# Grouped-query attention: the value product three steps behind its scores, the low half two steps behind

## The reference

```python
def gqa_dense(q, k, v, sink=None):
    scale = HEAD_DIM ** -0.5
    def attend(qb):
        s = jnp.einsum('bqhgd,bkhd->bhgqk', qb, k, preferred_element_type=F32) * scale
        ...
            p = jax.nn.softmax(s, axis=-1)
        return jnp.einsum('bhgqk,bkhd->bqhgd', p.astype(v.dtype), v)
    return sweep_queries(attend, (q,))
...
        elif kind == 1:
            q, k, vv, g_c = gqa_project(hc, gqa_w_in[j])
            q, k = rms_norm(q, gqa_q_norm[j]), rms_norm(k, gqa_k_norm[j])
            o_c = gqa_dense(q, k, vv)
            ...
            k_all = jnp.concatenate([cache_gqa_k[:, j], k_l], axis=1)
            v_all = jnp.concatenate([cache_gqa_v[:, j], v_l], axis=1)
            o_l = gqa_dense(q_l, k_all, v_all)
```

## Time and profile before

| | us |
|---|---|
| median of 3 runs | 4803.26 |
| lowest, highest | 4797.92, 4811.78 |
| the profiled execution | 4798.57 |
| its span | 4796.8 |
| TensorE busy in the span | 4166.2 (87%) |
| VectorE busy | 2699.8 (56%) |
| ACT busy | 2399.6 (50%) |
| GpSimd busy | 1178.5 (25%) |

### The profile page before, as it was taken

One profiled execution on the slowest core, in us unless ns is written; L12 is line 12 of the kernel. 1 busy time (PEld: TensorE's weight loads), 2 busy tenths in 40 slices (PEclk: granted clock), 3 DMA queues, 4 the chain that ended last, 5 costly groups with the idle time before them and its releaser, 6 DMA issues. The chain is left out here.

```text
span 4796.8 us, 63498 instructions
## 1 busy us (share of the span) xinstructions
PE 4166.2 (87%) x21676; PEld 2101.5 (44%) x21676; DVE 2699.8 (56%) x3564; ACT 2399.6 (50%) x3114; POOL 1178.5 (25%) x785
## 2 busy tenths in 40 slices
PE   5996899999958979999995978888859868999996
PEld 1443344444434444444443545555434433444443
DVE  4323577767345547777625516777453336777753
ACT  3324366666333227777723215666433245777752
POOL 1010143334211114444411201232210102444431
PEclk7997899999979979999997988999979988999998
DMA  4125422222111332222111333333111253222211
GB/s 177 51 70 156 112 60 69 62 63 59 31 47 49 95 92 70 69 69 69 46 31 44 102 96 80 87 83 88 45 40 56 67 152 91 50 49 49 49 35 57
DMA packets 372746, 343.63 MB, mean 72 GB/s; under 512 B 252576, under 2 KB 288992, under 8 KB 370944
## 3 DMA queue, kind: packets, MB, share of 16 engines
q1 hardware_dynamic: 372608, 341.81, 25.6%
HBM read 250.51 MB, written 91.23 MB: 71 GB/s over the span
## 5 line engine op out<-in xcount | busy, mean ns | idle before, releaser
L352 PE MATMUL bank<-H_hilo,w_hilo 128*128 128x512 f16 (+1 forms) x6336 | 1155.1, 345 | 25.9 <-DVE w_hilo L721 25.9
L1213 DVE TENSOR_REDUCE max_parts<-bank 128x1 f32<-128x512 f32 (+2 forms) x1536 | 953.5, 649 | 248.5 <-PE bank L1164 208.6
L1397 ACT ACTIVATE p_f<-bank 128x1024 f32<-128x1024 f32 (+2 forms) x768 | 741.8, 966 | 668.0 <-PE bank L1354 651.6
L1354 PE MATMUL bank<-q_slots,k_slots 96*128 96x512 f16 (+7 forms) x3968 | 957.8, 372 | 0.8 <-ACT p_hi L1401 0.6
L1469 DVE TENSOR_TENSOR p_lo<-p_f,p_hi 128x1024 f16<-128x1024 f32 (+2 forms) x624 | 738.2, 1186 | 341.1 <-ACT p_hi L1401 338.0
L352 PEld LDWEIGHTS bank<-H_hilo,w_hilo 128*128 128x128 f16 x6336 | 622.3, 98 | 558.3 <-DVE w_hilo L721 27.5
L1401 ACT ACTIVATE p_hi<-bank 128x1024 f16<-128x1024 f32 (+2 forms) x768 | 739.0, 962 | 0.0
L1164 PE MATMUL bank<-k_slots,q_slots 96*128 96x512 f16 (+4 forms) x1536 | 527.6, 381 | 110.5 <-DVE max_parts L1213 73.4
L1326 PE MATMUL bank<-p_hi,v_hi_ones 128*128 128x512 f16 (+2 forms) x1568 | 582.2, 372 | 10.2 <-DVE o_f L1449 6.8
L1328 PE MATMUL bank<-p_hi,v_lo_zeros 128*128 128x512 f16 (+2 forms) x1568 | 581.3, 371 | 0.0
L1330 PE MATMUL bank<-p_lo,v_hi_ones 128*128 128x512 f16 (+2 forms) x1568 | 579.2, 370 | 0.0
(11 more groups left out here) (140 smaller groups left out, 3856.1 us busy)
## 6 DMA issues: line engine op xcount, KB each, us to landing
ada_w<-in_w_ada SPq DMA_DIRECT2D x48, 768.0 KB, 5.6
k_slots<-k_gqa SPq DMA_DIRECT2D x96, 224.0 KB, 4.5
gate<-z_ring SPq DMA_DIRECT2D x32, 640.0 KB, 2.9
gate_rows<-gate SPq DMA_DIRECT2D x64, 320.0 KB, 3.9
q_slots<-q_mla SPq DMA_DIRECT2D x64, 240.0 KB, 3.1
k_mla<-hilo_out SPq DMA_DIRECT2D x64, 224.0 KB
k_slots<-k_mla SPq DMA_DIRECT2D x64, 224.0 KB, 4.3
v_hi_ones<-v_scratch SPq DMA_DIRECT2D x64, 224.0 KB, 2.9
```

Source lines behind the costliest of these rows:

```text
L352: ins = pe.matmul(dst, lhs(a, k), rhs(b, k), start=(k == 0 and n == 0), stop=(k == nk - 1 and n == 2))
L1213: dve.tensor_reduce(mx[:, par, t, c:c + 1], MB[(b * NE + k) % 2][:, 0:n], AX.X, ALU.max).then_inc(s_red.h, 1)
L1354: ins = pe.matmul(dst, lhs, rhs, start=(m == 0), stop=(m == len(ops) - 1), skip_group_check=swa)
L1397: act.activation(p32[:, p % 2, 0:cols], src, ACT.Exp, scale=scale).then_inc(s_p32.h, 1)
```

## The change

For layer 1 (`kind == 1`) a number `behind` is 3, for the others 2, as before. Where TensorE issued the value product of p-2 it issues that of p - behind; VectorE takes the low half of e = p - behind + 1 instead of p-1; the end of a unit on ACT, VectorE and the runs behind the last step move by the same one step. `ring(n)` gives a list of slots: n of them, or n + 1 over a stretch at the end of the pair where the number of steps asks for it. `p_hi` and `p_lo` get ring(4) in layer 1, which is 4 slots and for the last ten steps 5. `p_f32` gets ring(2). Since 26 is divisible by 2, ring(2) comes out with the two slots that there were. GpSimd's low halves and the layers 0, 2 and 3 stay as they were; line numbers grow by 6 or 7 behind the edit.

```diff
-        fours = next(n for n in range(P2) if (P2 - 4 * n) % 3 == 0)
-        slot = [p % 3 for p in range(P2 - 4 * fours)] + [p % 4 for p in range(4 * fours)]
-        back = [next(d for d in range(1, P2) if slot[p - d] == slot[p]) for p in range(P2)]
+        behind = 3 if kind == 1 else 2
+
+        def ring(n):
+
+            wide = next(m for m in range(P2) if (P2 - (n + 1) * m) % n == 0)
+            slots = [p % n for p in range(P2 - (n + 1) * wide)] + [p % (n + 1) for p in range((n + 1) * wide)]
+            return slots, [next(d for d in range(1, P2) if slots[p - d] == slots[p]) for p in range(P2)]
+        slot, back = ring(behind + 1)
+        ph = sb("p_hi", [P, max(slot) + 1, 1024], F16)
+        pl = sb("p_lo", [P, max(slot) + 1, 1024], F16)
+        slot32, back32 = ring(2) if behind > 2 else ([p % 2 for p in range(P2)], [2] * P2)
+        p32 = sb("p_f32", [P, max(slot32) + 1, 1024], F32)
...
-                        if (p >= 2 or not first) and (p < P2 or last):
-                            pv(i, p - 2)
+                        if (p >= behind or not first) and (p < P2 or last):
+                            pv(i, p - behind)
...
-                            if above_zero(g - 1):
-                                wait_lo(act, i, p - 2)
-                            act.activation(p32[:, p % 2, 0:cols], src, ACT.Exp, scale=scale).then_inc(s_p32.h, 1)
+                            if above_zero(g - back32[p] + 1):
+                                wait_lo(act, i, p - back32[p])
+                            act.activation(p32[:, slot32[p], 0:cols], src, ACT.Exp, scale=scale).then_inc(s_p32.h, 1)
...
-                        q = (p - 2) % P2
+                        q = (p - behind) % P2
...
-                    e = p - 3
+                    e = p - behind - 1
...
-                        if p <= P2 and not (first and p == 0) and (p - 1) % P2 % NS not in pooled:
-
-                            q = (p - 1) % P2
+                        e = p - behind + 1
+                        if e < P2 and not (first and e < 0) and e % P2 % NS not in pooled:
+
+                            q = e % P2
```

More of the change, by code:

```diff
@@ L993, in attention @@
         G = sb("gate_rows", [P, TOK], F32)
-        p32 = sb("p_f32", [P, 2, 1024], F32)
-        ph = sb("p_hi", [P, 4, 1024], F16)
-        pl = sb("p_lo", [P, 4, 1024], F16)
         mx = sb("max_parts", [P, 2, 4, 3], F32)
@@ L1338, in body @@
                 def body(i, first, last):
-                    for p in range(P2 + 2):
+                    for p in range(P2 + behind):
                         if p < P2:
@@ L1385, in body @@
                 def body(i, first, last):
-                    for p in range(P2 + (2 if last else 0)):
+                    for p in range(P2 + (behind if last else 0)):
                         if p < P2:
@@ L1405, in body @@
                                     copy_rows(act, i * 2 + b + 1, 1 - b, k)
-                        if p < 2 and first:
+                        if p < behind and first:
                             continue
-                        q = (p - 2) % P2
+                        q = (p - behind) % P2
                         u = steps[q % NS][0]
                         if q % NS == last_of[u]:
-                            un = 3 * (q // NS) + u - (6 if p < 2 else 0)
+                            un = 3 * (q // NS) + u - (6 if p < behind else 0)
                             b = q // NS
                             nq = units[u][1]
-                            act.wait_ge(s_av.h, s_av.base + i * P2 + p - 1)
+                            act.wait_ge(s_av.h, s_av.base + i * P2 + p - behind + 1)
                             if above_zero(i * 6 + un - 1):
@@ L1454, in body @@
                     i_first[0] = first
-                    for p in range(P2 + (3 if last else 0)):
+                    for p in range(P2 + (behind + 1 if last else 0)):
                         b = p // NS
@@ L1459, in body @@
                             take_entry(dve, i * 2 + b + 1, 1 - b, k)
-                        if p <= P2 and not (first and p == 0) and (p - 1) % P2 % NS not in pooled:
-                            q = (p - 1) % P2
+                        e = p - behind + 1
+                        if e < P2 and not (first and e < 0) and e % P2 % NS not in pooled:
+                            q = e % P2
                             cols = steps[q % NS][2]
-                            g = i * P2 + p - 1
+                            g = i * P2 + e
                             dve.wait_ge(s_ph.h, s_ph.base + g + 1)
@@ L1468, in body @@
                                 dve.wait_ge(s_av.h, s_av.base + g - back[q] + 1)
-                            dve.tensor_tensor(pl[:, slot[q], 0:cols], p32[:, q % 2, 0:cols], ph[:, slot[q], 0:cols],
+                            dve.tensor_tensor(pl[:, slot[q], 0:cols], p32[:, slot32[q], 0:cols], ph[:, slot[q], 0:cols],
                                               ALU.subtract).then_inc(s_pl.h, 1)
@@ L1528, in p_lo @@
                         pool.wait_ge(s_av.h, s_av.base + g - back[p] + 1)
-                    pool.tensor_tensor(pl[:, slot[p], 0:cols], p32[:, p % 2, 0:cols], ph[:, slot[p], 0:cols],
+                    pool.tensor_tensor(pl[:, slot[p], 0:cols], p32[:, slot32[p], 0:cols], ph[:, slot[p], 0:cols],
                                        ALU.subtract).then_inc(s_pp.h, 1)
```

## The result

The changed kernel takes 4904.79 us (median of 4 runs, 4902.59 to 4912.17) against 4804.24 for the kernel before in the same comparison: a ratio of 1.0211, 95% interval 1.0192 to 1.0230. It is 100 us slower, where 54 were forecast, and lies 7 us above the range that ended at 4898. The profiled execution took 4912.17, its span 4910.4.

The account below looks back on a forecast made before the run. TensorE was taken as close to full, 624 of 662 us; 43 us from waits and the moved product plus 12 for GpSimd, clock 0, made 55 us more: forecast 4857, range 4815 to 4898.

Parts of the forecast that it names:

- a(5): Step 5's max entry ahead of the value product on TensorE; forecast 11.9 after step 2's against 10.27, waiting for ACT's copy.
- The first value product: In step 3 of a head, TensorE was to wait for VectorE's division of unit 1, 1.4 us idle.
- the moved short product: Step 12's half-width value product moves to step 2, a full one to step 1: 0.65 more from a(11) to next a(2).
- from a(5) to a(11): TensorE from the first max entry of step 5 to that of step 11: 18.4 against 18.17, 0.25 more.
- The clock, taken as 0: TensorE's clock falls after idle pieces or ada: bounds -1.6 and +1.6 a head, -25 to +25 us; 0 in the sum.
- GpSimd beside VectorE, taken as 0.8 a head: VectorE's low halves held by GpSimd at lo(1), lo(2), lo(8): up to 1.7 a head; 0.8 taken, 12 us.
- lo(1): Low half of step 1 on VectorE, to start about 0.45 behind GpSimd's gate product of unit 1; bounds 0 and 0.8.
- lo(6): VectorE's low half of step 6, held up to 1.9 if GpSimd's of step 7 is first: 29 us more, 4887 to 4901.
- The copy comes in time: Rival: ACT reaches the turn's copy before a(5) is due and the change wins, 4752 to 4794; chance 0.06.
- The shift is absorbed: Rival: VectorE catches up during TensorE's idle time at a(5), 2.75 a head becomes 1 or less, 4803 to 4820; chance 0.12.
- full port waits or a second fall: Rival group: full port waits 4872, with lo(6) held 4887 to 4901; clock fall per new idle piece 4883; chance 0.22.
- The three waits announced: Signs: exponentials wait for VectorE's low half, step 5's max matmul about 2 us for the copy, first value product over 1 us.

Follow-up runs that it names:

- experiment 1: The changed kernel with ring(3) instead of ring(2) for `p_f32`, three slots and four at the end of the pair: 4816.72 us, ratio 1.0021.
- 2: The changed kernel with VectorE taking the low half of p-1 again, the value product still three steps behind: 4809.44 us, ratio 1.0012.
- 10: The changed kernel with ACT's copy of the turn ahead of its two exponentials in steps 4 and 8: 4828.60 us, ratio 1.0048.
- Experiment 8: The changed kernel with TensorE computing the scores of step 5 three times, 1.72 us more work a head: 4859.20 us, ratio 1.0114.
- experiment 4: The changed kernel with GpSimd's low half also waiting for VectorE's low half of the step before: 4864.32 us, ratio 1.0112.
- experiment 7: The kernel of 6 with VectorE's division at a unit's end ahead of the late maxima of its step: 4836.35 us, ratio 1.0063.
- 9: The changed kernel with step 5's scores computed three times and GpSimd's low half behind VectorE's of the step before: 4858.39 us, ratio 1.0105.
- 11: The kernel of 6 with the division early in step 2 alone and GpSimd's gate product of unit 1 held until lo(1) is done: 4809.48 us, ratio 1.0008.
- 6: The changed kernel with ring(3) for `p_f32` and GpSimd's low half behind VectorE's of the step before: 4809.90 us, ratio 1.0012.
- 12: The changed kernel with ACT's copies ahead of the exponentials and GpSimd's low half behind VectorE's of the step before: 4813.33 us, ratio 1.0016.

## Why the prediction was half right

**The mechanism held.** In the earlier trace rows a(5) came 10.27 after a(2); the working said 11.9, and it is 11.42, behind a wait of 1.81 for the copy (2.2 in the working; 2.44 in the other head of the pair). The first value product waits 1.30 for the division (1.4 in the working). From a(11) to the next a(2) it is 13.14, against 12.54 before: 0.60 for the moved short product, 0.65 in the working. Experiments 1, 2 and 10 confirm the cause from three sides: a slot more, the low half earlier, or the copy ahead of it takes away the loss at a(5).

**The step that failed is from a(5) to a(11).** The working had 18.4, the kernel takes 22.90. It lies in four places: a(5) to a(6) 4.51 where the working had 2.90; a(6) to a(7) 3.73 for 2.95; a(8) to a(9) 4.35 for 2.95; a(10) to a(11) 4.20 for 3.4. Two terms of the sum were too small.

*The clock, taken as 0.* The first of the four places is the matmuls at 0.63 in place of 0.38 and what follows at the same level, 1.6 us, in ten of eleven heads: the upper bound of the term. The idle pieces of 1.4 and 2.2 us had been named as what might bring it. Having written bounds of -1.6 and +1.6, I took the middle, although the very same sum put one idle piece of 2.2 us into each head and none of its terms took one away. Experiment 8 shows the size: filling that piece removes the fall, and 5→6 is 1.4 shorter although it holds more work. It also shows that the fall behind ada, which the kernel before has too, can be had back.

*GpSimd beside VectorE, taken as 0.8 a head.* At lo(1) and lo(2), where I looked for it, nothing is lost: both take 1.21, and it is GpSimd that gives way (2.73 instead of 1.26). lo(8) has its 0.45. But lo(4) and lo(6) follow GpSimd's own low halves and take 2.05 and 2.66. lo(6) stood among the rivals, as a race decided by 0.15 us; lo(4) stood nowhere, since the working let TensorE run through step 5 at full speed, by which VectorE would have been ahead. lo(9) is held too (2146.46, 3.07), but 11→12 is the same with and without that (5.88, and 5.90 in experiment 4). With GpSimd's low halves out of the way (experiment 4) 2.0 us a head come back. The head was forecast 2.75 + 0.8 = 3.55 longer and is 6.48 longer; the clock's 1.6 and the 1.2 by which 2.0 exceeds 0.8 are 2.8 of the missing 2.9. The full wait at lo(4) and lo(6) agrees with the Trainium skill, page "SBUF — State Buffer", section "Who interferes with whom": whoever has the shared port keeps it for the whole instruction. The traces add that VectorE's instruction ends 1.07 to 1.09 after GpSimd's, nearly its whole own length.

**The rivals.** "The copy comes in time" would decide only with a third slot, it said; with three slots and more (experiment 1) the copy is in time, and the kernel is still 0.2% slower than before, so the gain of up to 51 us isn't there. "The shift is absorbed" is out: nothing of the 6.5 us a head is made good later. The group "full port waits or a second fall" came true, and in a form that its prices left out: both together. Each was priced alone, 4883 and 4887 to 4901; with both, 25 + 29 on 4858, they give 4912, and 4904.79 was measured. That it comes so near is in part luck: lo(6) is held by 1.4 and not 1.9, and lo(4) by 0.8, which had no price. The range ended at 4898 because the two were treated as alternatives though one wait, the one at a(5), feeds both.

**What would show it.** The three waits announced are all there. For a head over 45 us the text named the POOL rows and the granted clock, and both answer yes.

**Open** is what decides whether a fall comes. In step 5 it isn't the length of the idle piece: the changed kernel has the fall behind 1.81 and behind 2.44 us, experiment 4 behind 1.81 only. Nor is it known why the lower level behind ada comes in every head of some kernels (before, after, 9), in two of three heads of 1 and 7, in about every other one of 10 and 11 and hardly ever in 6, 8 and 12. It isn't the idle time ahead of ada alone: 9 has less of it than 8 (8→11 is 9.10 and 10.42), and it is in 9 that the level falls. No experiment isolates it. In experiments 6, 7 and 11 a head without it has 12→2 at 6.5, one with it at 8.1 or more.

## What to carry to other kernels

When a wait moves to another place on an in-order engine, look for the smallest instruction that is queued behind it and ask who waits for that: here copies of 0.37 and 0.58 us, not the exponentials of 1 us, set off most of the loss, and moving them brought back 76 of 100 us. Price an idle piece of TensorE with the fall of the clock that may follow, and where two dear side effects have one cause, add them up in the range. A ring with n slots "or n + 1" has to be worked through for the number of steps at hand: with 26 steps ring(2) is still two slots.

## What was unexpected of the hardware

More work made the kernel faster. With 8 further score matmuls in each head, 1.72 us, experiment 8 is 45.6 us below the changed kernel, with a granted clock of 1.00 instead of 0.93 from 1890 to 2380 us.

Which of two engines gives way isn't told by the starts that the trace shows. With GpSimd's gate product shown 0.39 ahead, lo(1) passed unhindered (2114.53 and 2114.92); with GpSimd's low half 0.39 ahead, lo(4) was held in full (2080.57 and 2080.96, experiment 1); behind a gate product shown 0.42 ahead, a negation of 128x2 elements took 0.87 us instead of 0.17 (experiment 7). No experiment here tells what decides it.
